# A two-block transformer kernel on one core: the mixer of the second block rebuilt, with heads, norms and causal attention between projection blocks

## The reference

```python
def hybrid_layer(h, p_i, ...):                       # T = 256 tokens, D = 1024
    h = h + 0.5 * swiglu(rmsnorm(h, ffn1_norm), ...)
    u = rmsnorm(h, mix_norm)
    z = u @ w_in          # q,k 2048 | v 1024 | o 1024 | i 4 | f 4 | a_q 1024 | a_k 256 | a_v 256 | g_m 1024 | g_a 1024
    m_qk = silu(causal_dwconv(m_qk, m_conv_w, m_conv_b))         # 4 taps, 2048 channels
    hm = mlstm_chunkwise(mq, mk, mv, ig, lf)                     # 4 heads of 256, decayed causal scores
    hm = sigmoid(m_o) * head_rmsnorm(hm, m_out_norm)
    aq = head_rmsnorm(a_q, a_q_norm); ak = head_rmsnorm(a_k, a_k_norm)
    ha = swa_gqa_sinks(aq, ak, av, a_sinks)    # 16 query heads of 64, 4 key heads, causal window 128, sinks
    merged = sigmoid(g_m) * (hm @ w_branch_m) + sigmoid(g_a) * (ha @ w_branch_a)
    h = h + merged @ w_out
    h = h + 0.5 * swiglu(rmsnorm(h, ffn2_norm), ...)
    return h + sigmoid(rmsnorm(h, ple_norm) @ ple_gate_w) * (p_i @ ple_proj_w)
```

## Time and profile before

| | us |
|---|---|
| median of 3 runs | 2898.55 (2896.26 to 2901.74) |
| the profiled execution | 2892.88 |
| its span, first to last instruction | 2891.2 |
| PE busy | 2742.1 |
| DVE busy | 1894.6 |
| ACT busy | 556.7 |
| POOL busy | 123.6 |
| mean granted TensorE clock | 0.959 of full |

### The profile page before, as it was taken

The page is one execution under the profiler, slowest core; times in us unless marked ns, Lnnn a source line. Parts: engine busy times, 40 slices in busy tenths (PEclk is TensorE's granted clock), DMA queues, the critical chain, the costliest instruction groups (busy, mean ns, idle before and its releaser), DMA issues.

```text
span 2891.2 us, 34930 instructions
## 1 busy us (share of the span) xinstructions
PE 2742.1 (95%) x13475; PEld 2205.0 (76%) x13475; DVE 1894.6 (66%) x2189; ACT 556.7 (19%) x1208; POOL 123.6 (4%) x118
## 2 busy tenths in 40 slices
PE   6999999799997999899999989999989999999998
PEld 3777777577776775798787877788878887878887
DVE  3455456554447458887777867587677687766766
ACT  2111111311211146221110321210021013131101
POOL 0000000000000111100000001010000000000100
PEclk8999999899998999999999999699999999978999
DMA  6332422334343443554555435055455453523643
GB/s 247 131 109 80 158 104 88 99 131 175 111 155 123 162 109 74 162 190 160 181 171 179 153 119 201 30 177 186 162 176 181 154 179 131 175 88 106 203 164 133
DMA packets 251852, 420.67 MB, mean 145 GB/s; under 512 B 35576, under 2 KB 93376, under 8 KB 251680
## 3 DMA queue, kind: packets, MB, share of 16 engines
q1 hardware_dynamic: 247824, 410.09, 42.5%
q0 software_dynamic: 2720, 5.14, 0.6%
q10 hardware_dynamic: 1136, 3.12, 0.3%
HBM read 417.27 MB, written 1.05 MB: 145 GB/s over the span
## 4 chain that ended last, share of the span: by engine, by line
PE 60%; issue 29%; DVE 6%; POOL 2%; DMA 2%; ACT 1%; SPq 1%; ACTq 0%; POOLq 0%; DVEq 0%
PE psum L409 58%; PE psum L423 2%; POOL small L1909 2%; DVE wgt_lo L1311 1%; DVE wgt_hi L1309 1%; SPq L2000 1%; DMA raw<-ada_w 0%; DMA raw<-nat_w_in 0%; DMA raw<-mlp_w 0%; DVE psum L1555 0%; PE psum L633 0%; DVE n_probT L1566 0%; ACT W L922 0%; DVE psum L1392 0%; DVE small L1406 0%
## 5 line engine op out<-in xcount | busy, mean ns | idle before, releaser
L1311 DVE TENSOR_TENSOR wgt_lo<-raw,wgt_hi 128x2048 fp32r<-128x2048 f32 (+2 forms) x352 | 776.1, 2205 | 12.1
L409 PE MATMUL psum<-wgt_hi,xh 128*128 128x512 f32 (+2 forms) x1824 | 703.9, 386 | 11.6 <-DVE wgt_lo L1311 6.4
L409 PE MATMUL psum<-wgt_hi,xl 128*128 128x512 f32 (+2 forms) x1824 | 695.3, 381 | 0.0
L409 PE MATMUL psum<-wgt_lo,xh 128*128 128x512 f32 (+2 forms) x1824 | 694.8, 381 | 0.0
L1309 DVE CAST wgt_hi<-raw 128x2048 fp32r<-128x2048 f32 (+2 forms) x352 | 413.5, 1175 | 338.5 <-PE psum L409 139.1
L409 PEld LDWEIGHTS psum<-wgt_hi,xh 128*128 128x128 f32 x1824 | 346.9, 190 | 89.2 <-issue 17.8
L409 PEld LDWEIGHTS psum<-wgt_hi,xl 128*128 128x128 f32 x1824 | 346.6, 190 | 66.3
L409 PEld LDWEIGHTS psum<-wgt_lo,xh 128*128 128x128 f32 x1824 | 347.2, 190 | 64.8 <-issue 1.0
L409 PE MATMUL psum<-wgt_hi,yh 128*128 128x512 f32 x944 | 372.0, 394 | 7.5 <-DVE wgt_lo L1311 4.9
L409 PE MATMUL psum<-wgt_hi,yl 128*128 128x512 f32 x944 | 367.7, 390 | 0.0
L409 PE MATMUL psum<-wgt_lo,yh 128*128 128x512 f32 x944 | 367.5, 389 | 0.0
(11 more groups left out here) (175 smaller groups left out, 2044.2 us busy)
## 6 DMA issues: line engine op xcount, KB each, us to landing
raw<-mlp_w SPq DMA_DIRECT2D x64, 1024.0 KB, 5.3
raw<-w_in SPq DMA_DIRECT2D x60, 1024.0 KB, 4.9
raw<-ada_w SPq DMA_DIRECT2D x48, 1024.0 KB, 7.2
raw<-ffn_w_gate SPq DMA_DIRECT2D x40, 1024.0 KB, 5.1
raw<-ffn_w_up SPq DMA_DIRECT2D x40, 1024.0 KB, 5.1
raw<-ffn_w_down SPq DMA_DIRECT2D x40, 1024.0 KB, 4.9
raw<-ret_w_in SPq DMA_DIRECT2D x24, 1024.0 KB, 5.2
raw<-nat_w_in SPq DMA_DIRECT2D x12, 1024.0 KB, 5.8
```

What stands on the lines that cost most here:

```text
L409: return pe.matmul(o, l, r, start=start_, stop=stop, skip_group_check=True)
L1311: v.tensor_tensor(wgt_lo[:, s % RING, :size], r, wgt_hi[:, s % RING, :size], ALU.subtract).then_inc(split_done.sem, split_done.up())
```

## The change

- **Convolution:** eight pieces of two tiles (`conv(g, key)`, `qk_tile(g)`), chunks of `mq` in the order 0, 2, 1, 3, so that q and k of the first heads come first; `turn_qk` one block earlier; the pieces spread on DVE from the `mq` blocks to behind the gate rows, ACT's Silu piece by piece; each head waits only for its pieces.
- **Heads:** the scores of heads 0 and 1 stand before `gm`; after each `gm` block comes the values step of one head and the scores step of the head two further (`head_step`). Norms take both token tiles at once. The denominator comes from three one-column matmuls into a bank of its own (`md`), the values have 256 columns.
- **Order of the projections:** `gm`, `aq`, `ak`, then `hmT` and `bm`. The norms of aq and ak take both token tiles at once: three powers of 16 columns.
- **Attention:** six items of eight or four heads, each with two banks (even and odd heads). `ascores` adds the mask by an FP32R matmul with an identity and issues the heads of a pair behind one another, on rows 0 to 63 and 64 to 127. The values have the turned probabilities as the moving operand (256 columns) and write features by tokens, even heads to the upper and odd heads to the lower 64 partitions, so `haT` goes; the inverse of the denominator is spread by DVE, transposed (`ai`), copied by ACT, and multiplied in. These steps stand between the half blocks of `ga` (`in_gate`) and the blocks of `ba` (`in_branch`), and `ba` runs in the order (0,0), (1,0), (0,1), (1,1).
- **Ahead of the layer loop:** DVE waits for the mask table (`tri_in`) and makes rounded copies of mask and identity.

The diff, cut to its core:

```diff
-                                   after=lambda b: b > 1 and b % 2 and turn_qk(b // 2 - 1))
+                                   after=lambda b: b > 1 and b % 2 == 0 and turn_qk(b // 2 - 1), chunks=(0, 2, 1, 3))
...
-                    if h == 0:
-                        pe.wait_ge(conv_done.sem, conv_done.next())
+                    pe.wait_ge(conv_done.sem, conv_done.at((3, 4, 7, 8)[h]))
...
+                    o, d = open_unit(pe, ("mn", h), "val"), open_unit(pe, ("md", h), "dve")
...
-                            ins = mm(o[:, 0:MHD + 1], m_s[:, h % 2, lo:lo + P], v_ext[:, n, h, :], n == 0, n == tt)
...
-                for h in range(MH + 1):
-                    if h < MH:
-                        mscores(h)
-                    if h:
-                        mvalues(h - 1)
-                tokens_by_features("gm", KT, O_GM, D, range(2), x_op(xh), x_op(xl), "act", wb)
-                pe.wait_ge(out_of(("mn", MH - 1, 1)), emptied(("mn", MH - 1, 1)))
+                            s_ = m_s[:, h % 2, lo:lo + P]
+                            den = mm(d[:, tt:tt + 1], s_, ones, n == 0, n == tt)
+                            if n == tt == 1:
+                                close_unit(("md", h), den)
+                            ins = mm(o[:, tt * MHD:(tt + 1) * MHD], s_, v_tok[:, n, h * MHD:(h + 1) * MHD], n == 0, n == tt)
+                    close_unit(("mn", h), ins)
+                def head_step(h):
+                    mvalues(h)
+                    if h + 2 < MH:
+                        mscores(h + 2)
+                mscores(0)
+                mscores(1)
...
+                tokens_by_features("gm", KT, O_GM, D, range(2), x_op(xh), x_op(xl), "act", wb, after=head_step)
+                tokens_by_features("aq", KT, O_AQ, D, range(2), x_op(xh), x_op(xl), "dve", wb)
+                tokens_by_features("ak", KT, O_AK, BANK, range(2), x_op(xh), x_op(xl), "dve", wb)
+                pe.wait_ge(out_of(("mn", MH - 1)), emptied(("mn", MH - 1)))
                 ready = features_of("hmT", U, range(2))
                 tokens_by_features("bm", KT, 0, D, range(2), hid(yh, T), hid(yl, T), "dve",
                                    lambda *k: lblock(a["w_branch_m_2"], *k), ready=ready)
-                tokens_by_features("aq", KT, O_AQ, D, range(2), x_op(xh), x_op(xl), "dve", wb)
-                tokens_by_features("ak", KT, O_AK, BANK, range(2), x_op(xh), x_op(xl), "dve", wb)
...
                 def ascores(n):
+                    qt, c0, nh = a_heads(n)
+                    h0, w_ = c0 - 16 * qt, P * (qt + 1)
+                    outs = [open_unit(pe, ("as", n, j), "soft") for j in range(2)]
+                    mask = a_mask[:, P - qt * P:2 * P].unsqueeze(1).to_broadcast([P, nh // 2, w_])
+                    for o in outs:
+                        mm(o.rearrange("p (h k) -> p h k", h=nh // 2), ident_r, mask, True, False)
+                    for k in range(nh // 2):
+                        for j, o in enumerate(outs):
+                            h = h0 + 2 * k + j
+                            p0 = AHD * j
+                            ins = mm(o[:, k * w_:(k + 1) * w_], qT[p0:p0 + AHD, h // 2, qt * P:(qt + 1) * P], kT[p0:p0 + AHD, h // 4, 0:w_], False, True)
+                            if k == nh // 2 - 1:
+                                close_unit(("as", n, j), ins)
...
+                def aturn(n):
+                    qt = a_items[n][0]
+                    for j in range(2):
+                        pe.wait_ge(out_of(("as", n, j)), emptied(("as", n, j)))
+                        at = [i * P for i in range(4)] if qt == 0 else [i * 2 * P + s * P for s in range(2) for i in range(2)]
+                        transposes(("at", n, j), "dve" if j else "act", [a_buf(n, j)[:, lo:lo + P] for lo in at])
...
+                def ainverse(u):
+                    pe.wait_ge(ainv_ready.sem, ainv_ready.next())
+                    transposes(("ai", u), "act", [a_spread[:, k * P:(k + 1) * P] for k in range(4)])
...
+                    (qt, g), u = a_items[n], a_unit(n)
+                    key = ("ao", u)
+                    o = open_unit(pe, key, "val") if n % 3 < 2 else bank_of(key)
+                    for j in range(2):
+                        pe.wait_ge(out_of(("at", n, j)), emptied(("at", n, j)))
+                    for i in range(2):
+                        kv, s, lo = (2 * g + i, 0, i * T) if qt == 0 else (g, i, g % 2 * T)
+                        for j in range(2):
+                            ins = mm(o[AHD * j:AHD * (j + 1), lo:lo + T], av[:, s, kv * AHD:(kv + 1) * AHD], a_turned(n, j)[:, i * T:(i + 1) * T],
+                                     qt == 0 or s == 0, qt == 0 or s == 1)
+                    if a_last[u] == n:
                         close_unit(key, ins)
                         seen["a", n] = (psum_full, units[key]["full"])
                     else:
                         ins.then_inc(values_done.sem, values_done.up())
-                    seen["a", n] = (values_done, values_done.sent)
...
+                def in_gate(b):
+                    if b in (1, 3, 5, 7):
+                        aturn(b // 2)
+                    if b in (2, 4, 6):
+                        ascores(b // 2 + 1)
+                        if b != 4:
+                            ainverse(b // 4)
+                        avalues(b // 2 - 1)
+                def in_branch(b):
+                    if b == 0:
+                        aturn(4)
+                    if b == 1:
+                        avalues(4)
+                        aturn(5)
+                    if b == 2:
+                        ainverse(3)
+                        avalues(5)
+                    if b == 6:
+                        turn_x("mg", (0, 1), merged, ("ba", 0, 1))
+                ascores(0)
+                ascores(1)
+                tokens_by_features("ga", KT, O_GA, D, range(2), x_op(xh), x_op(xl), "act", wb, each=in_gate)
+                ascores(5)
+                ainverse(2)
+                avalues(3)
                 tokens_by_features("ba", KT, 0, D, range(2), hid(yh, T), hid(yl, T), "dve",
-                                   lambda *k: lblock(a["w_branch_a_2"], *k), ready=ready,
-                                   after=lambda b: b == 2 and turn_x("mg", (0, 1), merged, ("ba", 0, 1)))
+                                   lambda *k: lblock(a["w_branch_a_2"], *k), ready=lambda kt: ("ao", 1 if kt < 4 else 3),
+                                   order=[(0, 0), (1, 0), (0, 1), (1, 1)], each=in_branch)
                 tokens_by_features("wo", KT, 0, D, range(2), x_op(xh), x_op(xl), "dve",
                                    lambda *k: lblock(a["w_out_2"], *k), ready=pairs_of("mg"),
                                    mid=lambda: turn_x("mg", (2, 3), merged, ("ba", 1, 1)),
                 feed_forward(1, 1)
...
-                        for tt in range(TT):
-                            act.wait_ge(psum_full.sem, filled(("mq", c, tt)))
-                            act_(f_tok[c % 2][:, tt, :], bank_of(("mq", c, tt)), scale=rms[tt]).then_inc(act_out.sem, act_out.up())
-                    for g in (2 * c - 2, 2 * c - 1) if c else ():
...
+                def conv(g, key):
+                    keep_up(key)
+                    dve.wait_ge(out_of(("mqk", g)), emptied(("mqk", g)))
                     for j in range(CONV_K):
...
+                conv(0, ("mqk", 1))
+                conv(1, ("mq", 2, 1))
+                conv(2, ("mqk", 3))
+                conv(3, ("mq", 3, 1))
+                conv(4, ("mqk", 5))
...
+                conv(5, ("mv", 0, 1))
+                conv(6, ("mv", 1, 1))
...
                 v.tensor_scalar(rowv[6], rowv[6], -1.0, None, ALU.mult).then_inc(x_ready.sem, x_ready.up())
+                conv(7, ("mifT",))
                 keep_up(("mcol",))
...
+                for h in range(2):
+                    decay(h)
+                    scores(h)
+                for h in range(MH):
+                    denominators(h)
+                    if h + 2 < MH:
+                        decay(h + 2)
+                    variances(h)
+                    if h + 2 < MH:
+                        scores(h + 2)
+                    outputs(h)
...
+                softmax(0)
+                softmax(1)
+                aturned(0)
+                gate(0, 0)
+                ainverse(0)
+                gate(0, 1)
+                softmax(2)
+                aturned(1)
+                ahigh(0)
+                softmax(3)
+                aturned(2)
+                gate(1, 0)
+                ainverse(1)
+                softmax(4)
+                gate(1, 1)
+                aturned(3)
+                ahigh(1)
+                ainverse(2)
+                softmax(5)
+                aturned(4)
+                ahigh(2)
+                aturned(5)
+                ainverse(3)
+                ahigh(3)
...
+            dve.wait_ge(tri_in.sem, tri_in.at(16))
+            v.tensor_copy(a_mask, tri[:, P:3 * P])
```

(57 more changed lines are left out.)

493 lines of the change are left out of this document (238 added, 255 removed).

## The result

The changed kernel takes 2849.81 us, the median of four runs (2847.22 to 2853.18). Four runs of the kernel before, beside them, have a median of 2897.41. The ratio is 0.9835, 95% interval 0.9818 to 0.9852. The forecast was 2847, range 2822 to 2872.

A forecast was written before the change was run, and what follows sets the result against it. PE, busy 95% of the span, was the bound, so gains come from cheaper PE work, waits and half clock. Layers −26.6 and −28.2, once +3.7: −51.1 us, from 2898.55 to 2847, range 2822 to 2872.

The forecast's parts named there:

- mo term: mq to column transposes: convolution in eight pieces delays a mo split, PE waits; +2.4 us a layer, bounds 0 and +4.
- Heads: Heads between gm blocks: a 5.5 us block between a head's scores and values removes PE's waits; −6.8 us a layer.
- Convolution: Eight pieces: PE waits 3.2 us for the split behind piece 7, less about 0.8 in mv; +2.4 a layer.
- hmT and bm: Behind aq and ak: DVE's norms delay hmT's low parts, PE waits 8 us, slow matmuls add 2.3; +10.0 a layer.
- Rival A: Ahead of bm: the norms catch up, DVE reaches hmT with nothing behind, the 10.0 vanish; 2827 us, 15%.
- Attention: Pairs inside ga and ba: 70.2 us from first scores to wo at full clock; −32.2 in layer 1, −33.8 in layer 2.
- Rival C: Interleaved attention: the half clock stays through the stretch, making the kernel slower by 86 us; 2984 us, 4%.
- rival E: Interleaved attention: PE still waits out part of each item's chain, 4.3 us in each of six items; 2898 us, 4%.
- Without the blocks between it would stand on the path as now: Attention: DVE's part, 31.75 us today less mask additions, is hidden only by the blocks between the steps.
- Rival D: Attention on ACT: each Exp/Sigmoid switch holds ACT another 1.3 us, +2.6 a layer; 2852 us, 5%.
- The opening of the loop: Once, ahead of the layer loop: DVE waits for the mask table's DMA and makes two copies while PE idles; +3.7 us.

The follow-up runs named there:

- the run with the low parts early: Against the changed kernel, hmT's four low parts are made while ak's power is computed on GpSimd, ahead of ak's four products: 2843.80 us.
- the run with all edits: Changed kernel plus both norm edits, two mo splits ahead of the convolution's eighth piece, and mask wait and copies moved into the heads: 2815.46 us, ratio 0.9725.
- Two edits: Each alone against the changed kernel: splits asked for before aq's powers, 2845.06 us; hmT's low parts made during ak's power, 2843.80 us.
- the run on one half: Against the changed kernel, odd heads' scores also computed from rows 0 to 63 with even heads' data, so no row-half pairs; result partly changed: 2855.66 us.
- the run with the mo split: Against the changed kernel, DVE splits the third and fourth mo block ahead of the convolution's eighth piece, not behind it: 2837.19 us.

## Why the prediction was right, and where not

**The bound.** Right. Most of the gain is PE's waits and its clock; some 4 us a layer are cheaper work in the attention (an estimate, see above). The score pairs save 4.7 there, and the mask matmuls cost 3.7. By the rows the whole change gives 46.3 us where the sum has 51.1. The mo term is 6.0 us over the forecast in both layers together, and the heads of layer 2 gave 0.9 more than forecast.

**Heads.** The size was right (-6.8, measured -6.8 and -7.7). In layer 2 the wait of 5.6 us before had slow matmuls behind it, which went too. The reason was half wrong: the step "between the scores of a head and its values now lies a block of 5.5 us" names one of two covers, and DVE's order alone does as much.

**Convolution.** This is the term that was mis-sized: +2.4 with a bound of +4, measured +3.7 and +7.1. The mechanism was right, a wait for the split behind piece 7, but it was priced at 3.2 us and is 4.4 in both layers. And the slow matmuls behind the wait, 1.6 and 2.5 us, were priced for the 8 us wait, from rows 7 and 8, but not for this one. With them, the time from the first mo block to the column transposes grew by 6.3 and 7.1 us.

In layer 1, 2.6 of these came back ahead of mo: the split wait in mv of 0.8, as forecast, and the gate columns, which ran at nearly the full clock. In layer 2 nothing came back, since it had no split wait in mv before, and its gate columns and nine matmuls behind them (2365.6 to 2369.6) are slow as before. So the +3.7 is in part luck of this profile: in that of the run with the low parts early, whose code is the same up to there, layer 1 has 32.9 us from the gate columns to mo, where this profile has 29.6. In layer 1 the split ended 0.7 us before the forecast's count (1672.5, less the 6.6 us by which mq starts later, is 1665.9 against 1666.6) and PE came 1.7 before it. In layer 2, counted from mq, both came 3.2 us later than in layer 1, so the wait did not change.

**hmT and bm.** Right to 0.4: gm to bm 10.5 us against 10.3, then slow matmuls of 2.1 and 2.4 (bm's 96 against the same in the run with all edits) against 2.3. The table has 0.4 less, since bm's blocks before the change held 0.4 us more than those of that run. Two edits moved the wait by what the steps said. Rival A (15%) is out with 8.6 us of waiting for DVE: the power took 2.90 us, as extrapolated from rows 6.

**Attention.** 70.43 us against 70.2, partly by errors that cancel. A score item takes 1.6 to 1.75 us and not 1.5 (two mask matmuls take 0.55 to 0.66, not 0.46), and the waits sum to 0.65 and not 1.8: PE reached the values of item 3 at 41.5 us and not at 39.2, and waited 0.17 there. Score pairs at 1.07 us were met by 1.05. The bound for pairs that do not overlap was set too low, 1.7 where the run on one half has 1.95. The Trainium skill (TensorE: Matmul & The Clock Gate, Part 3: Packing small matmuls) lets tiles in different row groups end together; the run on one half agrees within a tenth, 1.07 against half of 1.95. Rival C (4%) is out at a clock of 1.00, and rival E (4%) with waits of 0.65 in all; but C not for the reason given: the forecast had argued with the dense blocks between, and the clock holds without them. "Without the blocks between it would stand on the path as now" was wrong: 5.8 us do.

**Table loads.** Rival D is out. ACT's rows between 1796.08 and 1866.51:

```profile
L990 ACT ACT_TABLE_LOAD x7 | 9.0, 1283 | 0.1
```

Seven loads of 1.28 us, with 0.1 us idle before them, and no wait of PE over 0.5 us. Where the Trainium skill (ScalarE: Activation LUTs, What ACT_TABLE_LOAD costs) puts 2.66 us on a switch, the trace has half of that.

**The opening of the loop.** +3.70, as forecast, and gone when the wait is moved.

## What to carry to other kernels

A long wait that PE no longer has can have two causes removed at once. Ask of each alone whether it would do, or one pays for cover that nothing needs. Price the slow matmuls behind every wait that shows a half clock behind its like, not behind the longest alone, and hold a stretch against the same code in several executions before its size is believed. Where an engine runs a queue of splits and norms, the cheap edits are those of order: what the busiest engine wants next goes ahead of what no one waits for yet, and work goes into a wait for a small operation elsewhere. Four such edits gave 34 us here, over two thirds of what the rebuilt mixer gave.

## What the hardware showed that was not expected

Four fp32 matmuls of 64 rows and 256 columns on two row halves take 1.07 us in the order A B A B and in A A B B, but eight of 128 columns take 1.09 and 1.64. On one half it is 1.93 to 1.97 for both.

A wait of 4.4 us was followed by 3.4 us at half clock in one layer and 5.3 in the other; behind 1.0 and 1.5 us there was none. Ahead of the first scores stands a wait of 1.65 us, behind 24 transposes: the changed kernel ran on at 1.00, but in layer 2 of the run with all edits and in layer 1 of the run with the mo split (1.68 us) the next 5.0 us had 0.66. The same code thus meets either clock. The kernel before ran 43 us at 0.51 with PE busy for 95% of them, where other orders of this work, with waits up to 2.0 and 1.3 us, ran at 0.94 and 1.00.
